# A two-block transformer layer in one kernel: three changes of order on ScalarE, VectorE and TensorE, and shorter groups of unread matmuls

## The reference, cut to what matters

```python
def swiglu(x, w1, w3, w2):
    return (jax.nn.silu(x @ w1) * (x @ w3)) @ w2
# first block
h = h + 0.5 * swiglu(rms_norm(h, ffn1_norm[l]), ffn1_w1[l], ffn1_w3[l], ffn1_w2[l])
gates = jax.nn.sigmoid(proj[..., o:o + N_BRANCHES * D_MODEL].reshape(B, S, N_BRANCHES, D_MODEL))
merged = gates[:, :, 0] * y_attn + gates[:, :, 1] * y_pool
h = h + 0.5 * swiglu(rms_norm(h, ffn2_norm[l]), ffn2_w1[l], ffn2_w3[l], ffn2_w2[l])
# second block, retention: q, k, v, g from one projection, then rotation of q and k
proj = u @ ret_w_in[i]
return jnp.concatenate([x1 * cos - x2 * sin, x1 * sin + x2 * cos], axis=-1)
```

## Time and profile before

| what | us |
|---|---|
| median of three runs | 1844.66 |
| lowest and highest | 1844.63, 1845.89 |
| the profiled execution | 1846.61 |
| its span in the trace | 1844.8 |

### The profile page before, as it was taken

The page is one execution under the profiler, slowest core; times in us unless marked ns, Lnnn a source line. Parts: engine busy times, 40 slices in busy tenths (PEclk is TensorE's granted clock), DMA queues, the critical chain, the costliest instruction groups (busy, mean ns, idle before and its releaser), DMA issues.

```text
span 1844.8 us, 28202 instructions
## 1 busy us (share of the span) xinstructions
PE 1829.5 (99%) x11335; PEld 1637.6 (89%) x11341; DVE 1396.1 (76%) x1912; ACT 929.3 (50%) x1274; POOL 81.5 (4%) x109
## 2 busy tenths in 40 slices
PE   9999999999999999999999999999999999999997
PEld 7998998888888988988998899988888888888886
DVE  8875887888778879866888887776777776666666
ACT  6652664435355536634653555455547644444445
POOL 0000000020001000000000000000000000000000
PEclk9999999999999999999999999999999999999999
DMA  6744763462407535743753778632231222222213
GB/s 214 180 124 131 198 166 111 175 154 70 120 24 205 154 114 142 195 149 108 195 148 101 195 211 241 225 135 78 105 137 62 78 92 69 91 80 79 91 69 91
DMA packets 60595, 244.78 MB, mean 133 GB/s; under 512 B 6865, under 2 KB 9457, under 8 KB 49857
## 3 DMA queue, kind: packets, MB, share of 16 engines
q1 hardware_dynamic: 46016, 199.25, 32.2%
q0 software_dynamic: 14032, 43.38, 12.5%
q10 hardware_dynamic: 432, 0.56, 0.1%
HBM read 223.76 MB, written 13.11 MB: 128 GB/s over the span
## 4 chain that ended last, share of the span: by engine, by line
PE 92%; DVE 4%; ACT 2%; DMA 1%; issue 1%; DVEq 0%; ACTq 0%; POOL 0%
PE acc L2573 17%; PE acc L2574 17%; PE acc L2575 17%; PE acc L2579 9%; PE acc L2581 9%; PE acc L2580 9%; PE att L2574 2%; PE att L2575 2%; PE att L2573 2%; PE att L2581 1%; PE att L2580 1%; PE att L2579 1%; DMA raw<-in_mix_seven 1%; PE acc L2848 1%; PE acc L2823 1%
## 5 line engine op out<-in xcount | busy, mean ns | idle before, releaser
L1457 DVE TENSOR_TENSOR w_lo<-raw,w_hi 128x2048 fp32r<-128x2048 f32 (+1 forms) x106 | 239.0, 2254 | 49.1 <-ACT w_hi L739 48.8
L739 ACT ACTIVATE w_hi<-raw 128x2048 fp32r<-128x2048 f32 (+1 forms) x106 | 199.3, 1880 | 75.3 <-PE acc L2575 61.4
L2573 PE MATMUL acc<-x_hi,w_hi 128*128 128x512 f32 x488 | 193.3, 396 | 0.3 <-DVE tmp L1685 0.3
L2579 PE MATMUL acc<-xt_hi,w_hi 128*128 128x256 f32 x684 | 190.0, 278 | 0.2 <-ACT tmp L838 0.2
L2575 PE MATMUL acc<-x_hi,w_lo 128*128 128x512 f32 x488 | 190.2, 390 | 0.0
L2574 PE MATMUL acc<-x_lo,w_hi 128*128 128x512 f32 x488 | 190.1, 390 | 0.0
L2581 PE MATMUL acc<-xt_hi,w_lo 128*128 128x256 f32 x684 | 189.5, 277 | 0.0
L2580 PE MATMUL acc<-xt_lo,w_hi 128*128 128x256 f32 x684 | 189.4, 277 | 0.0
L838 ACT ACTIVATE tmp<-acc 128x256 f32<-128x256 f32 x228 | 86.8, 381 | 123.7 <-PE acc L2581 116.4
L2573 PE MATMUL acc<-g_hi,w_hi 128*128 128x512 f32 x352 | 137.0, 389 | 0.0
L2575 PE MATMUL acc<-g_hi,w_lo 128*128 128x512 f32 x352 | 137.0, 389 | 0.0
(11 more groups left out here) (512 smaller groups left out, 5127.7 us busy)
## 6 DMA issues: line engine op xcount, KB each, us to landing
raw<-in_ffn_down SPq DMA_DIRECT2D x32, 704.0 KB, 4.1
raw_c<-in_ffn_seven SPq DMA_DIRECT2D x37, 512.0 KB, 5.0
raw<-in_ffn_seven SPq DMA_DIRECT2D x33, 512.0 KB, 4.8
raw<-in_ffn_seven POOLq DMA_DIRECT2D x33, 512.0 KB, 7.4
raw<-in_ffn_seven SPq DMA_DIRECT2D x37, 256.0 KB, 4.6
raw<-in_ret_values SPq DMA_DIRECT2D x8, 1024.0 KB, 4.8
raw<-in_ret_out SPq DMA_DIRECT2D x8, 1024.0 KB, 6.7
raw<-in_sb_v SPq DMA_DIRECT2D x8, 1024.0 KB, 4.8
```

Of the source, the lines that this page charges most:

```text
L739: nc.scalar.activation(w_hi[:, slot, at:at + cols], raw[:, slot, 0:cols], ACT.Copy).then_inc(w_hi_ready, 1)
L1457: tt(w_lo[:, slot, at:at + cols], raw[:, slot, 0:cols], w_hi[:, slot, at:at + cols].bitcast(F32), ALU.subtract).then_inc(w_ready, 1)
L2573: mm(dst, still[0], move[0], start=first, stop=False)
L2579: mm(dst, still[0], move[0], start=first, stop=False, skip_group_check=True)
```

## The change

ACT takes snap 3 in the last unit of a stretch ahead of `prep`. The turned rstd moves from behind unit 3 to behind all 14 units, and with it go DVE's copy and the banks' counts (one more bank is skipped in the norm's place). The first four operations of `rope_math(0)` move from unit 12 to unit 11. Groups of unread matmuls have two in place of three, and the first unit of each gate pair gets them too.

```diff
-UNREAD = 3
+UNREAD = 2
@@ ACT seven (feed-forward)
+                if not last:
+                    split_pair(ahead)
+                if since != 1:
+                    snap(3, t(1)[:, EARLY], two[:, EARLY])
                 if last:
                     prep()
                 else:
-                    split_pair(ahead)
-                if since != 1:
-                    snap(3, t(1)[:, EARLY], two[:, EARLY])
-                if not last:
                     split_one()
@@ ACT project_unit (retention)
-                if last:
-                    prep()
-                else:
+                if not last:
                     split_pair()
                 snap(3, t(1)[:, EARLY], two[:, EARLY])
                 if last:
+                    prep()
                     rope_split_b(0)
@@ ACT retention start
-            std_of(dst=4)
+            std_of(skip=1, dst=4)
@@ DVE project_unit
-                    b.next()
+                    b.next(2)
...
-                if i == TURN_AFTER + 1:
-                    turn_rstd(TB, freed=2)
...
+                if i == RET_SEVEN - 3:
+                    rope_products(0)
                 if i == RET_SEVEN - 2:
-                    rope_math(0)
+                    rope_sums()
@@ DVE behind the units
             unit_last(len(RET_UNITS) - 1)
+            turn_rstd(TB, freed=3)
@@ TensorE gates
-                    seven(6 if j == 1 and k == 0 else None, side)
+                    seven(6 if j == 1 and k == 0 else None, side, opens=k == 0)
@@ TensorE both_norms
-                mean_square()
+                mean_square(1)
@@ TensorE retention units
                 seven(12 if i == 0 else None, fourth=(t4_hi, t4_lo), opens=i == 0)
-                if i == TURN_AFTER:
-                    pe.wait_ge(att_free, b.at(BANKS - 1))
-                    turn_rstd(plain)
-                elif i == TURN_AFTER + 1:
-                    pe.wait_ge(att_free, b.at(BANKS))
+            pe.wait_ge(att_free, b.at(BANKS - 2))
+            turn_rstd(plain)
```

More of the change, by code:

```diff
@@ L76 @@
 RET_KEPT = len(RET_UNITS) - len(RET_STAY)
-TURN_AFTER = 3
 RET_OPS = 2 * RET_KC + TB + RET_VC
@@ L2118, in _, with rope_products @@
             ffn(FULL[1], gains[:, 2, :], gain_ret, gain_sq)
-            def rope_math(o):
+            def rope_products(o):
                 settle()
@@ L2130, in rope_math, with rope_sums @@
                 link(tt(t(5), x2, cos, ALU.mult))
+            def rope_sums():
                 tt(t(2), t(2), t(3), ALU.subtract).then_inc(val_ready, 1)
                 tt(t(4), t(4), t(5), ALU.add).then_inc(val_ready, 1)
+            def rope_math(o):
+                rope_products(o)
+                rope_sums()
             def rope_low_b(o):
```

## The result

The changed kernel takes 1861.2 us, the median of four runs (1860.33 to 1861.82). The kernel before took 1844.64 on the same chip (1842.36 to 1845.89). The ratio is 1.0086, 95% interval 1.0073 to 1.0099: slower by more than 0.2%. The forecast, 1838.3 us, was wrong. The first rival, that two unread matmuls don't turn the pace, gave 1857.7 and is what happened. The profiled execution took 1860.72 us, its span is 1858.9: +14.1 on the span of before.

What follows compares the result with a forecast made beforehand. TensorE, busy 99%, bounds the kernel by matmul count times start distance, quick 0.1133 or slow 0.1177 us. From 1844.7, terms -3.4 (turned rstd), -0.2 (rotation), -1.3 (snap 3), -1.2 (unread), -0.3 (gates) sum to -6.4: 1838.3 us, range 1836.2 to 1843.8.

Steps and rivals of the forecast that it cites:

- The first rival: 256-column stretches: two unread matmuls don't turn the pace, 38 units run slow; +13.0 us together, 1857.7 us; chance 0.12.
- two unread in place of three: Ten groups of unread matmuls lose one each: -1.2 us, if two are enough to turn the pace quick.
- one disturbance sets the pace: TensorE's 256-column stretches: one disturbance sets a lasting pace, 0.1133 or 0.1177 us between starts, 0.37 us per unit.
- 38 units x 0.37: Feed-forward and retention units, less slow beginnings and ends, that lose the quick pace if two unread fail: +14.2 us.
- the stalls of the rival's sum: Only the stalls saved at four feed-forward ends and in the retention layer: 4 x 0.17 + 0.2, -0.9 us.
- Turned rstd, -3.4: Retention layer: transposes moved behind all units leave 778 matmuls quick, 4.4 ns shorter each: -3.4 us, bounds 0 and -3.5.
- Snap 3, -1.3: Four feed-forward stretch ends: no stall or slow pace with snap 3 ahead of `prep`, -0.33 us each, `prep` in time.
- Rotation, -0.2: Retention unit 12: four products moved to unit 11 remove ACT's wait and TensorE's stall at 1180.48: -0.2 us.
- Gates, -0.3: Gate pairs: unread groups cost nothing in the first, turn the second and third quick, net -0.15 us each.
- A new wait in the retention layer: At the quick pace the accumulating DMA comes late or banks are short: 1839 to 1840 us; chance 0.07.

## Why the prediction was wrong

**The step that failed** is the one on two unread in place of three: "In the second group the distances change already between the first and the second matmul, as far as starts of 0.01 us tell it, so I think two are enough." The trace's starts in whole nanoseconds show that this is no sign. In the second product the first distances are 116 or 117 and then 121 or 122 ns, both with three and with two. With three it goes on 116, 114, 115, then 113; with two 116 to 118, then 118 for good. I read the start of a disturbance as the turn. And I had seen one number only; nothing in the trace of before could say that 3 works and 4 doesn't. The rival held the right case and I gave it 0.12. Also too strong was that one disturbance sets the pace: three in one product alone, or six in the first, left it slow.

**The rival's size.** It said +13.0; the spans say +14.1. The mis-sized term is "38 units x 0.37" = 14.2. The kernel before had 3389 quick matmuls in its eight stretches, 40.3 units, since the first gate pair (119) and the last 59 in retention were quick too. 3389 x 4.5 ns = 15.2; with -1.2 for ten groups, +1.4 for the three gate pairs and -0.9 for the stalls of the rival's sum and -0.5 for the one in the first gate pair it is +14.0. The medians on that chip differ by 16.6, because the profiled execution of before (1846.61) lies 2.0 us over its median of four, and that of the changed kernel 0.5 under its own. Beside the experiments the median of before is 1845.9 to 1846.6, and against these the loss is 14.6 to 15.3.

**Turned rstd, -3.4.** With three in both groups the retention stretch took 1182.93 - 1048.28 = 134.65 us, before 138.19: -3.5 with the rotation's -0.2. So the size was right, if the quick pace lasts. It lasted in that profile; the turned rstd alone gave -2.3, and three with the gates closed -1.3, by the stalls above. That they alone made it slow was too strong, as the run with snap 3 alone shows.

**Snap 3, -1.3.** Measured 0.35 an end where 0.33 was worked out. Right, and `prep` in time.

**Rotation, -0.2.** The wait of ACT and the stall at 1180.48 are gone. Right.

**Gates, -0.3.** With two: 28.48 a pair in place of 27.95, +0.53, of which the matmuls are 0.47. With three: +0.06. Wrong in sign, small.

**A new wait in the retention layer**, the last rival at 0.07, deserved more: it came in every profile that was quick behind unit 4, and never in the changed kernel itself. A slow unit gives the DMA 0.37 us more, but that doesn't rule the stall out: three in the second product alone, slow throughout, has one at 1185.80 (838 ns to the next start). Three in both groups gave -4.7 up to the values; what reaches the median is 0.0008 of 1845, 1.5 us (-0.2 to 3.3).

By the Trainium skill, page "TensorE: Matmul & The Clock Gate", section "Back-to-back issue gap", the gap of an isolated matmul when warm goes by its columns alone. The same section says that in a stream of weight loads and matmuls both set the spacing, which the prediction left out. The runs show what neither sentence has, two lasting spacings in one such stream: 299 or 311 matmuls in the same 35 us at granted clock 1.00, decided by three matmuls or two.

## What to carry to other kernels

Where a pace hangs on a cause that the trace shows without explaining, treat the number that works as given, and weigh a change of it by what the pace is worth (here 14 us) against what it saves (1.2). Count starts per window in every long stretch first: it shows in a minute which pace each stretch has, and durations don't (0.28 in both; the profile models the end of a matmul). And ask of every gain which DMA was only just in time: here late DMAs took back 2.7 of 4.7 us in one profile and 2.2 of 3.5 in another.

## What the runs showed that was not expected

- The number of inserted matmuls matters (three and six work, one, two and four don't), in two places one after the other, and with operands the other way round than those about them. Why is open.
- Stalls turn the pace either way, by the distances of the first two starts in ns. To slow: 168 and 227 (end of a feed-forward stretch), 149 and 224, 281 and 224, 324 and 222, 356 and 222, 807 and 226. To quick: 155 and 222, 215 and 223, 503 and 222, 1577 and 223. Left quick: 232 and 221. Left slow: 236 and 222, 838 and 225, 1380 and 224, 1760 and 224. I found no rule in the length.
- The second start behind each of these stalls is late, 0.22 to 0.23 us in place of 0.11, so such a stall costs some 0.11 more than its wait. Two small ones in slow stretches, 156 and 163 ns, had no late second start (118 and 119).
- The same kernel before had medians from 1844.6 to 1846.6 in four sets of runs, the last three on different chips; edits worth 1 us stayed unresolved here with ten runs of each.
